# Block products in three feed-forward stages, and modulation sums on GpSimd

## The chip, the core and the metric

The kernel runs on one core of one Trainium2 chip. The metric is the device time of one execution, in microseconds. Below, PE is TensorE, PEld its weight loads, DVE is VectorE, ACT is ScalarE, POOL is GpSimd and SP is SyncE, which issues the loads of weights.

## The reference, cut to what matters

A sequence of 512 tokens of width 1024 passes through three transformer blocks in float32. Four of their stages are feed-forward ones; three matter here:

- `f1` and `f2`, at the start and at the end of the first block: `h = silu(x @ w_gate) * (x @ w_up)` with a hidden width of 2816, then `x = layernorm(alpha * x + 0.5 * (h @ w_down))`.
- `mlp`, at the end of the third block: `h = square(relu(x @ w1))` with a hidden width of 4096, then `x + gate * (h @ w2)` and a norm.

The modulation of the third block is a small product beside them: `mod = silu(c) @ ada_w + ada_b`, with `ada_w` of 1024 x 6144. It does not depend on x, so the kernel works it out long before the third block.

## The kernel before, in words

**Precision.** Every float32 matrix product is made of three products of a faster type. x and each weight are cut into a high and a low half: ACT copies to a rounded type (`w_high`, line 431), DVE subtracts (`w_low`, line 443), and PE sums low times high, high times low and high times high (lines 467 and 646). x is kept turned (`x_high`, `x_low`: 8 blocks of 128 rows by 512 tokens).

**A plain tile.** A unit of weights is 1024 rows by 128 columns (512 KB). It is loaded into one of the 4 slots of a ring (line 415); SP issues the loads in order, and load c waits until what slot c - 4 held is used up. ACT and DVE cut it, and PE runs 24 matmuls of 512 columns into one bank. In `f1` all 22 gate tiles and 22 up tiles are plain, in `mlp` all 32.

**A block pair (class `Seven`, lines 510 to 704).** The gate tile and the up tile of the same 128 hidden columns share x. As a two by two block problem (K in two halves, tokens in two halves of 256, the two tiles as the other side) they need eight block products, and a scheme of Strassen and Winograd needs seven: 1 and 2 with x as it is, 6, 5, 7 and 3 with sums of x blocks (`SH`, `SL`, made once for the stage), 4 with x as it is, in the order 1, 2, 6, 5, 7, 3, 4. Each is 12 matmuls of 256 columns. The weights need sums as well: DVE makes `t21` (lines 618 and 620) and `t43` (lines 627 and 628), which are then cut like any unit, so a pair has four units: w1, t21, t43, and the second half of w2. ACT copies four partial results out of the banks (line 683), DVE adds them up (c11, c22, c12: lines 690, 696, 703) and multiplies (line 1225). In the kernel before, only `f2` does this, for 16 of its 22 pairs (j = 6 to 21); the first 6 are plain.

DVE works through a pair in a written order (`vector_ffn_seven`): low of t43(p), t21(p+1), c11(p), low of w22(p), low of w1(p+1), low of t21(p+1), t43(p+1), c22(p), c12(p), the multiplication. A chunk w1 of the ring is free once t43 is made from it, w2 once the low half of w22 is made.

**Modulation (class `Ada`).** `ada_w` comes in 12 column groups of 512, each in four chunks of 512 KB through the same ring: (group i, quarter q). Per chunk DVE does two `scalar_tensor_tensor` of 128x512 into an accumulator (line 965; the first of a group is a `tensor_scalar`), and after the fourth PE sums over the partitions with four small matmuls (line 978, a "column set"), which DVE adds to the bias. Groups 0 to 10 lie in `f1`, one chunk behind each of its 44 tiles, group 11 in the first four tiles of `f2`.

**POOL** in `f1` and `f2` issues the loads of the norm's rows, scales x by alpha in four instructions (line 1245), and is then idle to the end of the stage. In `mlp` it squares each tile out of `f_relu` (line 4354).

**The end of each stage** is the down product: its units rotate through the 3 places of `w_high`/`w_low` and through extra places laid over memory that is free by then (`Down.place`).

Of the kernel before, what the change touches and what calls it, by code (L numbers as in the profile page):

```python
# [968 lines left out]
def tensor_ada_columns(b, a, i, accs):  # L969
    if not 0 <= i < 12:  # L970
        return
    pe, acc = b.nc.tensor, accs[i % 2]
# [3 lines left out]
    pe.wait_ge(*a.g.dve.at("acc", i, 3))  # L976
# [158 lines left out]
def scalar_ffn(b, s):  # L1135
    ac, g, last = b.nc.scalar, s.g, len(s.order) - 1
    tokens = scalar_seven_tokens(b, s.seven) if s.seven else None
    for m, (what, j) in enumerate(s.order):
        if m == last - 1 and not s.seven:
            scalar_down_begin(b, g, s.down, hid_ready(s))  # L1140
        scalar_ahead(b, (s.tag, m), min(AHEAD, last - m) if s.seven else AHEAD)
        if s.seven and m >= last - 1:
# [4131 lines left out]
```

## Time and profile before

| | us |
|---|---|
| median of 3 runs | 3454.5 (3451.12 to 3454.76) |
| the profiled execution | 3452.42 |
| its span | 3451.2 |

The span runs from the first to the last instruction; the execution's own time is 1.2 us longer. The profile lists busy time by engine and, for chosen stretches, by window. `f1` is from 9 to 263 us before its down product, `f2` from about 1128 to 1351 us, `mlp` from 3092 to 3275 us.

### The profile page before, as it was taken

How to read it: one execution, taken by the hardware profiler on the slowest of the kernel's cores; microseconds unless marked ns; L12 is line 12 of the kernel's file. 1: busy time of each engine (PE TensorE's matmuls, PEld its weight loads, DVE VectorE, ACT ScalarE, POOL GpSimd, SP SyncE). 2: the span in 40 equal slices, each digit the busy share in tenths (PEclk: the TensorE clock that was granted, in tenths of full speed). 3: DMA queues.
4: the chain of work that ended last, by engine and by line, in shares of the span. 5: the costliest groups of instructions: out<-in, count | busy, mean ns of one | idle time of the engine just before them, and what ended most of it. 6: DMA issues, size and time to landing. Idle time of an engine off the chain costs nothing. (4 is left out here: it accounts for less than half of the span.)

```text
span 3451.2 us, 45725 instructions
## 1 busy us (share of the span) xinstructions
PE 3381.5 (98%) x17532; PEld 2837.8 (82%) x17532; DVE 2106.2 (61%) x3344; ACT 1495.7 (43%) x2717; POOL 334.4 (10%) x374
## 2 busy tenths in 40 slices
PE   8999999999999999999999999999999999999999
PEld 7887888886777899887887788887787888888887
DVE  5456565678546787763344576667476577672266
ACT  3225344345443355546223363346255243452354
POOL 1000200003000100023010100000000104222100
PEclk9999999999999999999999999999999999999999
DMA  6556421220224334620322243245411320143365
GB/s 242 189 184 213 144 68 56 85 87 25 91 93 158 116 105 155 199 79 13 110 81 87 68 135 99 96 165 165 121 38 31 115 91 26 38 141 98 105 201 165
DMA packets 107974, 386.30 MB, mean 112 GB/s; under 512 B 12060, under 2 KB 14764, under 8 KB 107504
## 3 DMA queue, kind: packets, MB, share of 16 engines
q1 hardware_dynamic: 101088, 364.86, 32.2%
q0 software_dynamic: 4528, 16.43, 1.6%
q8 instruction: 142, 2.33, 0.3%
q10 hardware_dynamic: 2144, 2.10, 0.2%
q14 instruction: 72, 0.59, 0.1%
HBM read 379.13 MB, written 4.21 MB: 111 GB/s over the span
## 5 line engine op out<-in xcount | busy, mean ns | idle before, releaser
L443 DVE TENSOR_TENSOR w_low<-ring,w_high 128x1024 fp32r<-128x1024 f32 (+2 forms) x519 | 650.8, 1256 | 701.7 <-ACT w_high L431 693.9
L467 PE MATMUL bank<-x_low,w_high 128*128 128x512 f32 (+1 forms) x2144 | 828.8, 390 | 16.4 <-DVE w_low L443 10.1
L467 PE MATMUL bank<-x_high,w_low 128*128 128x512 f32 (+1 forms) x2144 | 814.9, 384 | 0.0
L431 ACT ACTIVATE w_high<-ring 128x1024 fp32r<-128x1024 f32 (+2 forms) x519 | 538.0, 1038 | 592.3 <-PE bank L467 243.1
L467 PE MATMUL bank<-x_high,w_high 128*128 128x512 f32 (+1 forms) x2144 | 528.4, 384 | 0.0
L467 PEld LDWEIGHTS bank<-x_low,w_high 128*128 128x128 f32 x2144 | 404.7, 189 | 96.0 <-issue 16.1
L467 PEld LDWEIGHTS bank<-x_high,w_low 128*128 128x128 f32 x2144 | 405.0, 189 | 74.9 <-issue 3.6
L467 PEld LDWEIGHTS bank<-x_high,w_high 128*128 128x128 f32 x2144 | 388.1, 189 | 77.2 <-issue 4.8
L737 PE MATMUL bank<-w_low,x_high 128*128 128x512 f32 (+1 forms) x384 | 145.5, 379 | 2.5 <-ACT z_z L2076 1.5
L739 PE MATMUL bank<-w_high,x_high 128*128 128x512 f32 (+1 forms) x384 | 143.5, 374 | 0.0
L738 PE MATMUL bank<-w_high,x_low 128*128 128x512 f32 (+1 forms) x384 | 143.5, 374 | 0.0
L737 PEld LDWEIGHTS bank<-w_low,x_high 128*128 128x128 f32 x384 | 72.1, 188 | 18.6 <-DVE w_low L443 2.7
L402 POOL DMA_DIRECT2D const<-in_consts x3 | 1.8, 589 | 834.0 <-DVE x_low L920 361.9
L739 PEld LDWEIGHTS bank<-w_high,x_high 128*128 128x128 f32 x384 | 72.1, 188 | 12.7
L738 PEld LDWEIGHTS bank<-w_high,x_low 128*128 128x128 f32 x384 | 72.1, 188 | 12.3 <-issue 0.2
L3061 ACT ACTIVATE c_in<-bank 128x512 f32<-128x512 f32 x44 | 26.4, 599 | 101.3 <-PE bank L467 101.2
L4335 ACT ACTIVATE f_relu<-bank 128x512 f32<-128x512 f32 x32 | 19.1, 598 | 116.6 <-PE bank L467 116.6
L3084 DVE SCALAR_TENSOR_TENSOR c_y<-c_in,cols,c_y 128x512 f32<-128x512 f32 x88 | 66.2, 752 | 3.1
L965 DVE SCALAR_TENSOR_TENSOR f_ada<-ring,cond,f_ada 128x512 f32<-128x512 f32 x84 | 65.4, 778 | 2.8
L851 PE MATMUL bank<-w_low,c2d_in 128*128 128x512 f32 x168 | 65.7, 391 | 0.0
L853 PE MATMUL bank<-w_high,c2d_in 128*128 128x512 f32 x168 | 65.4, 389 | 0.0
L852 PE MATMUL bank<-w_high,c2d_in 128*128 128x512 f32 x168 | 65.3, 389 | 0.0
(746 smaller groups left out, 6917.8 us busy)
## 6 DMA issues: line engine op xcount, KB each, us to landing
ring<-in_W SPq DMA_DIRECT2D x686, 512.0 KB, 3.5
X<-in_x POOLq DMA_DIRECT2D x1, 2048.0 KB, 10.9
x_spill<-X POOLq DMA_DIRECT2D x1, 2048.0 KB, 8.3
X<-x_spill POOLq DMA_DIRECT2D x4, 512.0 KB, 3.6
ring<-in_W SPq DMA_DIRECT2D x4, 432.0 KB, 3.2
out<-X SPq DMA_DIRECT2D x3, 512.0 KB, 5.0
const<-in_consts POOLq DMA_DIRECT2D x1, 1133.0 KB, 10.6
f_hid<-in_xT ACTq DMA_DIRECT2D x4, 256.0 KB, 8.1
```

Of the source, the lines that this page charges most:

```text
L431: ac.activation(b.UH[u.place][:, 0:u.K * u.n], u.src(), ACT.Copy).then_inc(*b.split.act.up("high", i))
L443: dv.tensor_tensor(b.UL[u.place][:, 0:n], u.src(), b.UH[u.place][:, 0:n].bitcast(F32), SUB).then_inc(*b.split.dve.up("low", i))
L467: i = pe.matmul(out, w[:, k, c], v, start=n == 0 and q == 0, stop=last and q == 3 * K - 1)
L737: pe.matmul(out, xh, wl[:, q, :], start=k + q == 0, stop=False)
L738: pe.matmul(out, xl, wh[:, q, :], start=False, stop=False)
L739: i = pe.matmul(out, xh, wh[:, q, :], start=False, stop=k + q == 7)
L851: pe.matmul(out, u[:, 0, s], wl[:, 0, c], start=k == 0, stop=False)
L852: pe.matmul(out, u[:, 1, s], wh[:, 0, c], start=False, stop=False)
L853: x = pe.matmul(out, u[:, 0, s], wh[:, 0, c], start=False, stop=k == d.nk - 1)
L965: x = dv.scalar_tensor_tensor(acc, w[:, k, :], b.cond[:, 2 * q + k:2 * q + k + 1], acc, MUL, ADD)
L3061: ac.activation(s.cb[m % 3][:, 2:514], b.bk["c2u", m], ACT.Copy).then_inc(*g.act.up("copied", m))
L3084: dv.scalar_tensor_tensor(y, x[:, q:q + 512], b.col("ffn_conv_w_2", 44 * q + c), y, MUL, ADD).then_inc(*(g.dve.up("conv", m) if q == 2 els ...
```

## The change

- `f1` and `mlp` use block pairs too: `f1` has 6 plain pairs and 16 block pairs as `f2` has, `mlp` has 6 plain tiles and then 13 pairs of neighbouring tiles (j and j + 1).
- In `mlp` POOL makes the four whole blocks of x that the sums need, DVE the sums; the relu of a pair is done in place in `hid` by three ACT instructions, and POOL squares the pair's two tiles in place behind the last of them. The operands of the last product (`Down.H`), the norm's row and the places of `mlp` lie over the memory of the sums, and wait for the last pair's products. The norm's row is loaded behind the last pair.
- Modulation: `f1` has groups 0 to 5, `f2` groups 6 to 11. The first two groups of each stage ("early") are summed on DVE beside the first 8 plain tiles as before. The other four ("late") are summed on POOL, one chunk per block pair: per quarter chunk row block a `tensor_scalar` into `product` and a `tensor_tensor` that adds it to the accumulator, both of 128x512. Their column sets stand behind pairs 5, 9 and 13, the last one in the down product. Accumulator and product lie in the memory of the norm's rows, so these are loaded when the last column set is done.
- The ring's order in the block pairs of `f1` and `f2` is now w1, w2, modulation chunk, so w2(p+1) needs the slot of w1(p), and w1(p+1) needs the slot of modulation chunk p - 1.

```diff
+def gpsimd_ada_step(b, a, i, q, acc, tmp, over):
+
+    gp, w = b.nc.gpsimd, b.w(("ada", i, q))
+    gp.wait_ge(*b.loaded(("ada", i, q)))
+    if q == 0:
+        gp.wait_ge(*a.g.act.at("cond"))
+        if over is not None:
+            gp.wait_ge(*a.g.pe.at("columns", over))
+        gp.tensor_scalar(acc, w[:, 0, :], b.cond[:, 0:1], None, MUL).then_inc(*a.pool.up())
+    for k in range(0 if q else 1, 2):
+        gp.tensor_scalar(tmp, w[:, k, :], b.cond[:, 2 * q + k:2 * q + k + 1], None, MUL).then_inc(*a.pool.up())
+        gp.wait_ge(*a.pool.now())
+        x = gp.tensor_tensor(acc, acc, tmp, ADD)
+        x.then_inc(*(a.pool.up("acc", i, q) if k else a.pool.up()))
+        gp.wait_ge(*a.pool.now())
+
...
+PLAIN = 3
...
+        self.acc = {i: copies[:, 512 * (n % 2):512 * (n % 2) + 512] for n, i in enumerate(early)}
+        self.acc.update({i: self.G[:, 0, 512 * (n % 2):512 * (n % 2) + 512] for n, i in enumerate(late)})
+        self.over = {i: x[n - 2] if n > 1 else None for x in (early, late) for n, i in enumerate(x)}
+        self.product = self.G[:, 1, 0:512]
...
+        self.seven = Seven(b, Area(b, self.end), self.g, f"{tag}s", copies)
...
+    def early_steps(self, m):
+
+        return [(self.early[m // 4], m % 4)] if 0 <= m < 4 * len(self.early) else []
+
+    def early_columns(self, m):
+
+        return {7: self.early[:1], 11: self.early[1:]}.get(m, [])
+
+    def late_columns(self, p):
+
+        return self.late[(p - 5) // 4] if p in (5, 9, 13) else None
...
 def ffn_units(b, s, before=None):
     s.first = FIRST if before else NU
+    last = len(s.order) - 1
     for m, (what, j) in enumerate(s.order):
         b.unit((s.tag, m), (s.pre + "_w_gate", s.pre + "_w_up"), down_rows(8), [(j * 128 + what * 2816, 128)],
                lambda m=m: s.g.pe.at(s.tag, m))
-        for q in (m - 1,) if 0 < m < 43 else (42, 43) if m == 43 else ():
-            ada_chunk(b, s.ada, s.ada_from + q // 4, q % 4)
+        for q in (m - 1, m) if m == last else (m - 1,):
+            for step in s.early_steps(q):
+                ada_chunk(b, s.ada, *step)
         if before and m == FIRST - 1:
             leave_places(b, before)
     for j in range(s.plain, 22):
         seven_units(b, s.seven, (s.pre + "_w_gate", s.pre + "_w_up"), j * 128, 2816 + j * 128)
+        p = j - s.plain
+        if p < 4 * len(s.late):
+            ada_chunk(b, s.ada, s.late[p // 4], p % 4)
     down_units(b, s.g, s.down, s.pre + "_w_down")
-    if s.seven:
-        s.down.added.append(s.seven.added)
+    s.down.added.append(s.seven.added)
...
-        if m % 4 == 3 and m > 3:
-            tensor_ada_columns(b, s.ada, s.ada_from + m // 4 - 1, s.acc)
+        for i in s.early_columns(m):
+            tensor_ada_columns(b, s.ada, i, s.acc[i])
     for p in range(22 - s.plain):
         tag = s.seven.tag
         tensor_seven(b, s.seven, p, {"p": g.act.at("silu", s.plain + p), "q": g.dve.at(tag, "c11", p),
                                      "r": g.dve.at(tag, "c12", p)})
+        i = s.late_columns(p)
+        if i is not None:
+            tensor_ada_columns(b, s.ada, i, s.acc[i])
...
 def gpsimd_ffn(b, s, ready):
     gp, g = b.nc.gpsimd, s.g
-    for i, what in enumerate("gb"):
-        gp.dma_start(s.G[:, i, :], b.io[f"{s.norm}_{what}"].partition_broadcast(128)).then_inc(
-            b.load_sem(f"{s.norm}{what}"), 16)
     for t in range(4):
         for r in ready(t):
             gp.wait_ge(*r)
         gp.tensor_scalar(b.X[:, t, :], b.X[:, t, :], ALPHA, None, MUL).then_inc(*g.pool.up("alpha", t))
+    for i in s.late:
+        for q in range(4):
+            gpsimd_ada_step(b, s.ada, i, q, s.acc[i], s.product, s.over[i])
+    gp.wait_ge(*s.ada.g.pe.at("columns", s.late[-1]))
+    for i, what in enumerate("gb"):
+        gp.dma_start(s.G[:, i, :], b.io[f"{s.norm}_{what}"].partition_broadcast(128)).then_inc(
+            b.load_sem(f"{s.norm}{what}"), 16)
...
-    for m in range(32):
+    for m in range(SINGLE):
...
+    for m in range(SINGLE, 32, 2):
+        seven_units(b, s.seven, "mlp_w1_3", 128 * m, 128 * m + 128)
...
+SINGLE = 6
+LAST_PAIR = (32 - SINGLE) // 2 - 1
...
+def gpsimd_mlp_whole(b, s, n):
+
+    i, j = ((0, 0), (1, 0), (1, 1), (0, 1))[n]
+    b.nc.gpsimd.tensor_tensor(s.seven.work[n], block(b.XH, i, j).bitcast(F32), block(b.XL, i, j).bitcast(F32),
+                              ADD).then_inc(*s.gm.pool.up("whole", n))
...
+def scalar_mlp_pair(b, s, p):
+    ac, g, v, j = b.nc.scalar, s.gm, s.seven, SINGLE + 2 * p
+    scalar_ahead(b, (v.tag, "t43", p), 0)
+    if p == 0:
+        ac.wait_ge(*g.pool.at("hid", SINGLE - 1))
+    scalar_seven_copy(b, v, p, "a", 1, "p", "c11")
+    scalar_ahead(b, (v.tag, "w22", p), 0)
+    scalar_ahead(b, mlp_behind(s, p, 0), 0)
+    scalar_seven_copy(b, v, p, "b", 6, "p", "c12")
+    scalar_seven_copy(b, v, p, "d", 5, "r", "c22")
+    if p == LAST_PAIR:
+        scalar_down_begin(b, s.gf, s.downf, mlp_ready(s))
+    scalar_ahead(b, mlp_behind(s, p, 1), 0)
+    scalar_seven_copy(b, v, p, "c", 7, "p", "c22")
+    x = s.hid[:, j, 0:256]
+    ac.wait_ge(*g.dve.at(v.tag, "c11", p))
+    ac.activation(x, x, ACT.Relu).then_inc(*g.act.up())
+    ac.wait_ge(*g.pe.at(v.tag, 4, p))
+    ac.activation(s.hid[:, j, 256:512], b.bk[v.tag, "p", p][:, 0:256], ACT.Relu).then_inc(*g.act.up(v.tag, "c21", p))
+    x = s.hid[:, j + 1, :]
+    ac.wait_ge(*g.dve.at(v.tag, "c12", p))
+    ac.activation(x, x, ACT.Relu).then_inc(*g.act.up("pair", p))
...
+def vector_mlp_pair(b, s, p):
+    v, j = s.seven, SINGLE + 2 * p
+    vector_ahead(b, (v.tag, "t43", p), 0)
+    if p < LAST_PAIR:
+        vector_seven_t21(b, v, p + 1)
+    if p == LAST_PAIR:
+        b.nc.vector.wait_ge(*b.split.dve.at("low", b.unit_of[v.tag, "t43", p]))
+    vector_seven_c11(b, v, p, s.hid[:, j, 0:256])
+    vector_ahead(b, (v.tag, "w22", p), 0)
+    vector_ahead(b, mlp_behind(s, p, 1), 0)
+    if p < LAST_PAIR:
+        vector_seven_t43(b, v, p + 1)
+    vector_seven_c22(b, v, p, s.hid[:, j + 1, 256:512])
+    vector_seven_c12(b, v, p, s.hid[:, j + 1, 0:256])
+    if p == LAST_PAIR:
+        vector_down_begin(b, s.gf, s.downf)
...
+    for p in range(LAST_PAIR + 1):
+        gp.wait_ge(*g.act.at("pair", p))
+        for j in (SINGLE + 2 * p, SINGLE + 2 * p + 1):
+            x = s.hid[:, j, :]
+            gp.tensor_tensor(x, x, x, MUL).then_inc(*g.pool.up("hid", j))
+    gp.wait_ge(*g.pe.at(s.seven.tag, 4, LAST_PAIR))
+    gp.dma_start(s.GF, b.io["final_g_3"].partition_broadcast(128)).then_inc(b.load_sem("final_g_3"), 16)
...
-        self.f1 = Ffn(b, self.ada, "f1", "ffn1", "ln1", 0)
+        self.f1 = Ffn(b, self.ada, "f1", "ffn1", "ln1", [0, 1], [2, 3, 4, 5])
+        self.ada.pool = self.f1.g.pool
         self.staged = self.f1.hid[:, 14:22, :]
         self.m1 = Mix1(b)
-        self.f2 = Ffn(b, self.ada, "f2", "ffn2", "ln3", 11, 3)
+        self.f2 = Ffn(b, self.ada, "f2", "ffn2", "ln3", [6, 7], [8, 9, 10, 11])
...
```

## Rows read from the trace of the kernel before

**Rows 1.** Part 1 of the page: busy time of each engine.
```profile
PE 3381.5 (98%) x17532; PEld 2837.8 (82%) x17532; DVE 2106.2 (61%) x3344; ACT 1495.7 (43%) x2717; POOL 334.4 (10%) x374
```

**Rows 2.** Windows: us, busy us (count) of PE, PEld, DVE, ACT, POOL, clock, DMA.
```profile
59.22:240.92 181.70, 181.70 (x834) 151.30 (x834) 94.17 (x121) 42.63 (x48) 0.00 (x0) 1.00 0.51 185
1204.90:1341.60 136.70, 136.70 (x1179) 136.70 (x1178) 119.91 (x169) 80.02 (x140) 0.00 (x0) 1.00 0.34 109
```

**Rows 3.** Chain that ended last, in order of time: start us, us, what.
```profile
3017.40 27.22 PE bank L467 x120
```

**Rows 4.** Timeline of DVE in one block pair: start us, us, what, idle before.
```profile
1202.33 1.23 DVE L443 TENSOR_TENSOR w_low<-f2s_t,w_high 128x1024 fp32r<-128x1024 f32 x1 [1.53 <-ACT w_high L431]
1203.59 0.69 DVE L627 TENSOR_TENSOR f2s_t<-ring,f2s_t 128x512 f32<-128x512 f32 x1
1204.20 0.68 DVE L628 TENSOR_TENSOR f2s_t<-ring 128x512 f32<-128x512 f32 x1
1204.80 0.42 DVE L696 TENSOR_TENSOR f_hid<-f_ada 128x256 f32<-128x256 f32 x1
1205.13 0.42 DVE L703 TENSOR_TENSOR f_hid<-bank,f_ada 128x256 f32<-128x256 f32 x1
1205.59 0.69 DVE L1225 TENSOR_TENSOR f_hid<-f_hid,f_gate 128x512 f32<-128x512 f32 x1
1206.47 1.23 DVE L443 TENSOR_TENSOR w_low<-f2s_t,w_high 128x1024 fp32r<-128x1024 f32 x1 [0.18 <-ACT w_high L431]
1207.83 0.69 DVE L618 TENSOR_TENSOR f2s_t<-ring,ring 128x512 f32<-128x512 f32 x1
1208.56 0.69 DVE L620 TENSOR_TENSOR f2s_t<-ring,f2s_t 128x512 f32<-128x512 f32 x1
1209.16 0.42 DVE L690 TENSOR_TENSOR f_gate<-bank,f_ada 128x256 f32<-128x256 f32 x1
1209.50 0.68 DVE L443 TENSOR_TENSOR w_low<-ring,w_high 128x512 fp32r<-128x512 f32 x1
1210.10 1.22 DVE L443 TENSOR_TENSOR f2s_unit<-ring,f2s_unit 128x1024 fp32r<-128x1024 f32 x1
1212.15 1.23 DVE L443 TENSOR_TENSOR w_low<-f2s_t,w_high 128x1024 fp32r<-128x1024 f32 x1 [0.83 <-ACT w_high L431]
```

**Rows 5.** Timeline of PE in the next block pair (product 3, next product 1).
```profile
1211.88 0.28 PE L646 MATMUL bank<-f2s_sl,w_high 128*128 128x256 f32 x1
...
1214.66 0.28 PE L646 MATMUL bank<-x_low,f2s_unit 128*128 128x256 f32 x1
```

**Rows 6.** Page, part 6: one load of the ring, KB, us to landing.
```profile
ring<-in_W SPq DMA_DIRECT2D x686, 512.0 KB, 3.5
```

**Rows 7.** Timelines at 1020 us: an adding instruction of POOL beside DVE.
```profile
1020.24 1.29 POOL L1422 TENSOR_TENSOR m_merged<-m_merged,bs_part 128x512 f32<-128x512 f32 x1 [8.76 <-DVE bs_part L1409]
...
1020.62 1.99 DVE L443 TENSOR_TENSOR w_low<-ring,w_high 128x1024 fp32r<-128x1024 f32 x1 [0.46 <-ACT w_high L431]
```

**Rows 8.** Timelines of the first stage, POOL beside DVE at 28 and 32 us.
```profile
28.34 2.80 POOL L1245 TENSOR_SCALAR X<-X 128x1024 f32<-128x1024 f32 x1 [8.95 <-DMA X<-in_x]
...
28.34 1.59 DVE L965 SCALAR_TENSOR_TENSOR f_ada<-ring,cond,f_ada 128x512 f32<-128x512 f32 x1
...
31.12 2.76 POOL L1245 TENSOR_SCALAR X<-X 128x1024 f32<-128x1024 f32 x1
...
32.23 1.23 DVE L443 TENSOR_TENSOR w_low<-ring,w_high 128x1024 fp32r<-128x1024 f32 x1 [1.51 <-ACT w_high L431]
```

**Rows 9.** Source line 965: duration ns min/median/max, first and last start, forms.
```profile
L965 DVE SCALAR_TENSOR_TENSOR f_ada<-ring,cond,f_ada x84: 741/752/1592, 20.0 to 1154.9; 128x512 f32<-128x512 f32 x84
```

**Rows 10.** Source line 4354: the squares on POOL in the third stage.
```profile
L4354 POOL TENSOR_TENSOR f_hid<-f_relu x32: 1031/1042/1042, 3110.0 to 3270.9; 128x512 f32<-128x512 f32 x32
```

**Rows 11.** Timeline of ACT behind product 4 of a block pair.
```profile
1205.11 0.38 ACT L1178 ACTIVATE f_gate<-bank 128x256 f32<-128x256 f32 x1 [2.09 <-PE bank L646]
1205.39 1.05 ACT L431 ACTIVATE w_high<-f2s_t 128x1024 fp32r<-128x1024 f32 x1
```

More of the change, by code:

```diff
@@ L515, in __init__ @@
         self.SL = area.take(f"{tag}_sl", 4, 4, 256, dtype=F32R, past=3 * LINE)
-        self.T = area.take(f"{tag}_t", 1024)
-        area = place_area or area
+        self.T = area.take(f"{tag}_t", 1024) if T is None else T
         over = Area(b, area.at)
-        self.place = [area.take(f"{tag}_unit", SLOT, dtype=F32R) for _ in range(2)]
-        self.work = [self.T.rearrange("p (k c) -> p k c", k=4)] + [over.take(f"{tag}_x", 4, 256) for _ in range(2)]
+        self.place = [area.take(f"{tag}_unit", SLOT, dtype=F32R, past=LINE) for _ in range(2)]
+        self.work = list(work) or [four(self.T)] + [over.take(f"{tag}_x", 4, 256) for _ in range(2)]
         self.copy = {x: copies[:, 256 * i:256 * i + 256] for i, x in enumerate("abcd")}
@@ L975, in tensor_ada_columns @@
         pe.wait_ge(*e)
[L976 removed]
+    pe.wait_ge(*a.acc(i, 3))
     for j in range(4):
@@ L1136, in scalar_ffn @@
     ac, g, last = b.nc.scalar, s.g, len(s.order) - 1
-    tokens = scalar_seven_tokens(b, s.seven) if s.seven else None
+    tokens = scalar_seven_tokens(b, s.seven)
     for m, (what, j) in enumerate(s.order):
[L1139 to L1142, printed above, removed]
+        scalar_ahead(b, (s.tag, m), min(AHEAD, last - m))
+        if m >= last - 1:
             scalar_seven_start(b, s.seven, m == last)
@@ L1220, in vector_ffn_seven @@
             vector_seven_t43(b, v, p + 1)
+        for i in s.early_columns(len(s.order) - 1) if p == 0 else ():
+            vector_ada_columns(b, s.ada, i)
+        i = s.late_columns(p - 1)
+        if i is not None:
+            vector_ada_columns(b, s.ada, i)
         vector_seven_c22(b, v, p, s.hid[:, j, 256:512])
@@ L4323, in tensor_mlp, with vector_mlp_sum, summed, scalar_mlp_high @@
         tensor_tile(b, g, ("f3u", m), [("f3u", m)], 0, b.x, bank.ap)
-def scalar_mlp(b, s):
-    ac, g = b.nc.scalar, s.gm
-    for m in range(32):
-        if m == 30:
-            scalar_down_begin(b, s.gf, s.downf, mlp_ready(s))
-        scalar_ahead(b, ("f3u", m))
+    for p in range(LAST_PAIR + 1):
+        tensor_seven(b, s.seven, p, {"p": g.act.at(tag, "c21", p), "q": g.dve.at(tag, "c11", p),
+                                     "r": g.dve.at(tag, "c12", p)})
+def gpsimd_mlp_whole(b, s, n):
+    i, j = ((0, 0), (1, 0), (1, 1), (0, 1))[n]
+    b.nc.gpsimd.tensor_tensor(s.seven.work[n], block(b.XH, i, j).bitcast(F32), block(b.XL, i, j).bitcast(F32),
+                              ADD).then_inc(*s.gm.pool.up("whole", n))
+def vector_mlp_sum(b, s, i):
+    dv, g, f, tag, (w0, w1, w2, w3, w4) = b.nc.vector, s.gm, s.gm.dve, s.seven.tag, s.seven.work
+    out, one, two, op, n = {2: (w4, w0, w1, SUB, 1), 0: (w1, w1, w2, ADD, 2), 1: (w0, w1, w0, SUB, 2),
+                            3: (w3, w3, w0, SUB, 3)}[i]
+    dv.wait_ge(*g.pool.at("whole", n))
+    if i != 2:
+        dv.wait_ge(*f.now())
+    dv.tensor_tensor(out, one, two, op).then_inc(*f.up(tag, "sum", i))
+def summed(s, i):
+    w0, w1, w2, w3, w4 = s.seven.work
+    return {2: w4, 0: w1, 1: w0, 3: w3}[i]
+def scalar_mlp_high(b, s, i):
+    ac, g, v = b.nc.scalar, s.gm, s.seven
+    ac.wait_ge(*g.dve.at(v.tag, "sum", i))
+    ac.activation(v.SH[:, i, :, :], summed(s, i), ACT.Copy).then_inc(*g.act.up(v.tag, "high", i))
+def vector_mlp_low(b, s, i):
+    dv, g, v = b.nc.vector, s.gm, s.seven
+    dv.wait_ge(*g.act.at(v.tag, "high", i))
+    dv.tensor_tensor(v.SL[:, i, :, :], summed(s, i), v.SH[:, i, :, :].bitcast(F32),
+                     SUB).then_inc(*g.dve.up(v.tag, "low", i))
+def scalar_mlp(b, s):
+    ac, g, v, last = b.nc.scalar, s.gm, s.seven, SINGLE - 1
+    for m in range(SINGLE):
+        scalar_ahead(b, ("f3u", m), min(AHEAD, last - m))
+        if m >= last - 1:
+            scalar_ahead(b, (v.tag, "t21" if m == last else "w1", 0), 0)
         ac.wait_ge(*g.pe.at("f3u", m))
@@ L4338, in mlp_ready @@
 def mlp_ready(s):
-    return lambda k: [s.gm.pool.at("hid", k)]
+    g, tag = s.gm, s.seven.tag
+    return lambda k: [g.pool.at("hid", k)] + ([g.pe.at(tag, 5 if k < 3 else 4, LAST_PAIR)] if k < 4 else [])
 def vector_mlp(b, s):
-    for m in range(32):
-        vector_ahead(b, ("f3u", m))
-        if m == 30:
-            vector_down_begin(b, s.gf, s.downf)
+    dv, g, v, last = b.nc.vector, s.gm, s.seven, SINGLE - 1
+    sums, lows = {1: (2,), 2: (0, 1), 3: (3,)}, {4: (2, 0), 5: (1, 3)}
+    for m in range(SINGLE):
+        vector_ahead(b, ("f3u", m), min(AHEAD, last - m))
+        for i in sums.get(m, ()):
+            vector_mlp_sum(b, s, i)
+        if m == last - 2:
+            dv.wait_ge(*g.pe.at("f3u", FIRST - 1))
+            vector_seven_t21(b, v, 0)
+        for i in lows.get(m, ()):
+            vector_mlp_low(b, s, i)
+        if m >= last - 1:
+            vector_ahead(b, (v.tag, "t21" if m == last else "w1", 0), 0)
```

129 lines of the change are left out of this document (70 added, 59 removed).

## The prediction

> **What bounds the kernel now.** I read part 1 of the page first: PE is busy for 98% of the span [rows 1]. So only what takes work off PE, or makes PE wait, moves the time. Then I compared two stretches by window: in the plain tiles of `f1` and in the block pairs of `f2` PE is busy without a gap, at the full clock (1.00, the 2.4 GHz level), while POOL does nothing at all [rows 2]. What differs is DVE: 94.17 of 181.70 us in the plain tiles, although modulation runs on it, but 119.91 of 136.70 us, 88%, in the block pairs. So the block pair is cheaper on PE and is close to being bound by DVE. The reader is to see in the timeline of one pair how little is left: two idle pieces, 0.83 and 0.18 us [rows 4].
>
> **What a pair costs.** Plain: five tiles (120 matmuls) take 27.22 us in the chain [rows 3], so 5.44 a tile, 10.89 a pair. Block pair: 14 of them in 136.70 us [rows 2] are 9.76 each. The change turns 16 pairs of `f1` and 13 pairs of `mlp` into block pairs: if nothing else moved, that would be 29 x 1.13 = 32.7 us off PE. The column sets of modulation: the first stretch of rows 2 is 8 times four tiles with one set, 22.71 us each, less 4 x 5.444 = 21.78 leaves 0.93 us a set. There are 12 before and after.
>
> **What is added, and where.** In 16 pairs of `f1` and in 16 of `f2`, POOL sums a modulation chunk: two `tensor_scalar` and two adding `tensor_tensor` of 128x512 (a first quarter has one of the latter, so 1.75 on average). Alone they would be nothing to PE. The question is what they do to DVE, whose 88% I have just named. The rows on this:
> - An adding instruction of POOL of this size and form takes 1.29 us. DVE's low half begins 0.38 us after it and takes 1.99 instead of 1.23 [rows 7, 4]: it is held up for 0.76, until 1.14 us after POOL's start. So an add holds DVE off for 1.14 us.
> - A `tensor_scalar` of 128x1024 takes 2.80 us. DVE's `f_ada` instruction that starts with it takes 1.59 instead of 0.75 [rows 8, 9], so it is held off for 0.84 us, but a low half that starts 1.1 us after the next one takes 1.23 as if alone [rows 8]. Half the size: an estimate of 0.42 us.
> - The instructions that suffer read two operands from SBUF. In a block pair that is all of DVE's work but c11 and c12, which read a bank [rows 4].
>
> The Trainium skill ("SBUF — State Buffer", section "Who interferes with whom") says that DVE with two SBUF inputs and a GpSimd instruction that reads SBUF contend for one shared pair of ports, and that the one which comes second fully blocks. It speaks of a lock for the whole instruction; the low half at 32.23 us, 1.23 long inside a 2.76 us instruction of POOL, disagrees with "whole" [rows 8], the add agrees nearly. It is a rule against this change, and its full form is rival D.
>
> So per chunk POOL holds DVE off for up to 2 x 0.42 + 1.75 x 1.14 = 2.84 us. DVE's own work in a pair, from start to start with the two idle pieces taken out, is 9.76 - 1.01 = 8.75 [rows 2, 4]. Were all of the hold-off paid: 11.6 us. Part of it falls beside c11, c12 (0.34 each from start to start) and the short waits between dependent instructions, and part of an instruction's hold is hidden when DVE's next start would come later anyway. Walking POOL's four instructions through rows 4 from the landing of a chunk, I get 2.3 for a chunk with four and 1.6 for a first quarter: 2.15 on average. **Period P in `f1` and `f2`: 8.75 + 2.15 = 10.9 us**, taken as 10.95 with small change; bounds 9.76 (all hidden) and 11.6 (none). DVE is then what ends last: PE waits for the low half of w22, product 3's weights. Today that half ends at 1210.18 (1209.50 + 0.68) and product 3 begins at 1211.88 [rows 4, 5], so DVE can fall behind by 1.7 us once before PE waits.
>
> Nothing else is late in this loop: ACT has the room, and a load takes 3.5 us [rows 6]. w2 of the pair after next is issued when t43 is made (1204.20 + 0.68) and would land at 1208.4, 0.6 us after t21 starts today (1207.83) [rows 4]; the 0.83 of idle covers it, and in a DVE-bound pair the hold-off between the two does. POOL needs some 2 x (1.4 + 1.3) = 5.4 us for a chunk and with its own blocking some 7.5, less than a period, so its slot of the ring comes back in time.
>
> **The sum.** The first chunk of a stage is summed before pair 0, so 15 periods are stretched: 15 x (10.95 - 9.76) - 1.7 = 16.1 us per stage.
> - `f1`: 16 x 9.76 + 16.1 - 16 x 10.89 = -1.9 us.
> - `f2`: already block pairs, so the loss alone: +16.1 us.
> - Column sets: the three late ones of each stage stand where PE waits for DVE, so 6 x 0.93 = 5.6 us are hidden: -5.6 us.
> - `mlp`: no modulation, but two squares a pair. One takes 1.04 us [rows 10] and holds DVE off by an estimated 0.9. DVE has no multiplication here, so its work is 8.75 - 0.8 = 7.95. The longest loop: behind product 4 (0.0) relu of the bank to 0.6, of the second tile 0.6 to 1.2 (one of 128x512, an estimate from 0.38 for half of it), high of t43 to 2.3 [rows 11], the second square in the way until 3.2, low 4.4, t21 5.8, c11 6.1, w22 low 6.8, and product 3 wants it at 1211.88 - 1204.90 = 6.98. It just fits; I take 9.80 a pair: 13 x (10.89 - 9.80) = -14.2 us. At worst the loop overruns: 10.5 a pair, -5.1.
> - Start and end of `mlp`: eight splits of sums on ACT and DVE have 13.8 us of PE work (two tiles, two products) in front of product 6 and need some 11; at the end ACT cuts three operands before the last copy c, about 0.5 us late. +1.5 in all, bounds 0 and 6. In `f1` and `f2` the start is that of `f2` today, where PE goes from plain tiles into pairs without a gap; four more modulation steps on DVE (1.5 us each) lie in plain tiles with DVE half free. 0.
> - Loads of the norm's rows later, extra places that wait for the last products, POOL's four whole blocks: 0, each with tens of us of down product or tiles over it; bound 1.
>
> -1.9 + 16.1 - 5.6 - 14.2 + 1.5 = **-4.1 us**. The terms are differences inside the span (3451.2), to which the execution adds 1.2: 3452.4 - 4.1 = 3448.3. The median of the runs is 2.1 above that execution (0.06%): **3450.4 us**. This is a draw: 0.2%, 6.9 us, is about the least that a measurement of this kernel can tell from no change. By P the total goes as 30 us per us of period (15 x 2), and it crosses zero at P = 11.1.
>
> **The rivals.**
> - **A. POOL mostly hides (faster).** If POOL's instructions come to run where DVE is waiting anyway, or find gaps between its instructions without holding it, P falls to 9.76 to 10.5. For it: 1.01 idle per pair, and both engines are regular. Against: one add alone is longer than both idle pieces. At 10.3: 15 x 0.54 - 1.7 = 6.4 a stage: -11.6 + 6.4 - 5.6 - 12.7 = -23.5, 3431 us. With no contention at all the sets are not hidden: -18.1 + 0 - 14.7 + 1.5 = -31, 3423 us.
> - **B. The hold-offs are paid in full (slower).** The mechanism is that DVE's instructions stand one behind the other, so that each hold shifts all that follow; P = 8.75 + 2.84 = 11.6, and `mlp` overruns too (10.5). 15 x 1.84 - 1.7 = 25.9: +7.9 + 25.9 - 5.6 - 5.1 + 1.5 = +24.6, 3479 us; with `mlp` at 9.80, 3470. It decides from P = 11.1. For it: the rows show DVE instructions delayed by the full remainder of POOL's hold. Against: c11, c12 and the waits must hide something.
> - **C. The change hardly does what it says on DVE:** if the chunk's slot came back late, w1 and w2 would land late and the ring would set the period. Its price is the excess over 3 us of margin; the trace of before can't show POOL's duration under load. It adds to B; 12 us a period would be +27 us, 3481.
> - **D. The other's whole instruction.** 2 x 1.4 + 1.75 x 1.29 = 5.1 a chunk, less 0.5: P = 13.3, 51 us a stage: +34 + 51 - 5.6 - 12.7 = +67, 3521 us. The rule of the skill's page named above, taken literally, gives it; rows 8 speak against it.
>
> **How the numbers follow.** The forecast (P between 10.7 and 11.3, 3443 to 3461) 0.35; A 0.34; B 0.24; C 0.04; D 0.03. The range leaves out no contention at all (3423), C's tail and D: 3427 to 3477. Faster by over 0.2% (under 3447.6): all of A and a small part of the forecast, 0.37; slower (over 3461.4): B, C, D, 0.32; within, 0.31.
>
> **What would show it.** In the profile after: windows over the block pairs of `f1` and `f2` should give some 10.95 us a pair with DVE at 95% or more and PE at about 89%; PE idle before products of line 646 should be put down to DVE line 443 (`w_low<-ring`, w22). The mean of DVE's `tensor_tensor` with two SBUF operands there should be up by about a quarter, c11 and c12 unchanged. `mlp` should be at 9.8 a pair without gaps. I would be wrong in the mechanism if PE had no idle in these pairs, if its waits were for ACT or the ring, or if `mlp`'s block pairs were the slow ones.

## The result and the profile after

The changed kernel takes **3474.7 us** (median of 6 runs, 3471.3 to 3477.7) against 3454.2 for the kernel before (6 runs beside it). The ratio is 1.0059, with a 95% interval of 1.0048 to 1.0070: slower by 20.5 us. The forecast was 3450, a draw.

Part 1 of the page, to be read beside [rows 1]: PE is busy for 9.4 us less, yet the span is 21.6 us longer (3472.8). So PE has 31 us more without work. POOL has 246 us more work.
```profile
PE 3372.1 (97%) x18576; PEld 2871.4 (83%) x18576; DVE 2305.8 (66%) x3561; ACT 1590.8 (46%) x2928; POOL 580.0 (17%) x498
```
Windows over 14 block pairs of `f1`, 14 of `f2` and 11 of `mlp` (columns as in [rows 2]):
```profile
93.35:248.09 154.74, 145.06 (x1202) 143.19 (x1201) 140.24 (x172) 80.29 (x140) 94.97 (x53) 0.98 0.42 144
1204.71:1358.85 154.14, 142.83 (x1202) 140.15 (x1201) 141.74 (x172) 80.44 (x140) 98.01 (x53) 1.00 0.44 145
3166.53:3278.49 111.96, 110.85 (x926) 108.88 (x925) 91.46 (x120) 67.26 (x121) 33.33 (x22) 1.00 0.33 104
```
A pair of `f2` took 9.76 in the kernel before. It now takes 154.14 / 14 = 11.01, one of `f1` 11.05 and one of `mlp` 10.18 (111.96 / 11). These are means: by the starts of product 1, single pairs of `f1` take 9.8 to 13.6 and of `f2` 9.8 to 12.0. DVE is busy 140.24 / 14 = 10.02 us per pair instead of 119.91 / 14 = 8.57 [rows 2], for the same instructions. But it isn't busy all the time: 14.5 us of the first window are idle. What ended the idle time over much the same stretch of `f1` (engine, what waited, for what; us in total, times, longest):
```profile
POOL f_norm L977 <- DMA ring<-in_W: 62.3, 12, 17.2
...
DVE f1s_t L617 <- DMA ring<-in_W: 11.0, 10, 2.4
PE bank L645 <- DVE w_low L443: 9.5, 8, 1.9
```
PE waits for the low half of w22, as forecast. DVE itself waits for t21, which needs w2 from the ring. That wait was not in the forecast. A stretch of DVE in `f1` shows both (start us, us, what, idle before), to be read beside [rows 4]:
```profile
159.54 0.69 DVE L627 TENSOR_TENSOR f1s_t<-ring 128x512 f32<-128x512 f32 x1
...
161.65 1.21 DVE L443 TENSOR_TENSOR w_low<-f1s_t,w_high 128x1024 fp32r<-128x1024 f32 x1
164.51 0.84 DVE L617 TENSOR_TENSOR f1s_t<-ring,ring 128x512 f32<-128x512 f32 x1 [1.65 <-DMA ring<-in_W]
...
166.33 1.44 DVE L443 TENSOR_TENSOR w_low<-ring,w_high 128x512 fp32r<-128x512 f32 x1
167.69 1.21 DVE L443 TENSOR_TENSOR f1s_unit<-ring,f1s_unit 128x1024 fp32r<-128x1024 f32 x1
...
188.76 2.31 DVE L443 TENSOR_TENSOR f1s_unit<-ring,f1s_unit 128x1024 fp32r<-128x1024 f32 x1
```
and POOL beside it:
```profile
162.15 1.87 POOL L979 TENSOR_TENSOR f_norm<-f_norm 128x512 f32<-128x512 f32 x1
164.12 1.57 POOL L977 TENSOR_SCALAR f_norm<-ring,cond 128x512 f32<-128x512 f32 x1
165.77 1.45 POOL L979 TENSOR_TENSOR f_norm<-f_norm 128x512 f32<-128x512 f32 x1
...
188.33 1.66 POOL L979 TENSOR_TENSOR f_norm<-f_norm 128x512 f32<-128x512 f32 x1
```
The load of w2 goes out when t43 is made (159.54 + 0.69 = 160.23, SP's issue is at 160.25) and lands at 164.43, so it takes 4.2 us. DVE is ready 1.65 us earlier, at 162.86, since little held it off between t43 and t21: POOL is at work there too, but t43's low half takes 1.21, what it takes alone. The next three loads of w2 took 4.9, 3.4 and 3.6 us, and even behind the one of 3.4 DVE waited 0.95. Then the low half at 166.33 takes 1.44 instead of 0.68, beside an add of POOL, and the one at 188.76 takes 2.31 instead of 1.22.

The longest pair of `f1`, 13.6 us, has a wait of PE of 1.90 us that ends at 123.70. PE's matmuls then start 0.12 us apart to 124.7, 0.21 apart to 127.9 and 0.12 apart again, and the granted clock shows it (columns as above):
```profile
124.00:128.00 4.00, 4.00 (x25) 4.00 (x24) 3.79 (x6) 0.00 (x0) 0.92 (x1) 0.62 0.69 262
```

**Ledger** of the two profiled executions, by first matmuls (us; difference after minus before):

| stretch | before | after | difference | forecast |
|---|---|---|---|---|
| start to first product of `f1`'s down | 254.5 | 248.8 | -5.7 | } |
| `f1`'s down product | 125.4 | 128.0 | +2.6 | } |
| to the first block pair of `f2` | 806.1 | 807.6 | +1.5 | } +8.6 |
| 16 block pairs of `f2` | 156.1 | 175.1 | +19.0 | } |
| `f2`'s down product | 122.5 | 124.3 | +1.8 | } |
| from there to `mlp` | | | -0.1 | 0 |
| `mlp`'s tiles and pairs | 178.6 | 179.2 | +0.6 | -12.7 |
| `mlp`'s down product | 173.9 | 176.2 | +2.3 | 0 |

Five column sets (0.93 each) that stood in the first row's stretch before stand in `f2` now: one right ahead of its first block pair (at 1192.67, so in the third row), three in its pairs and one in its down product. The rows sum to +22.0, with marks slightly inside the span's ends.

### The profile page after: what moved, and what is told of

It is laid out like the page before. It is cut to its first block and busy times, and to the rows that moved or that the text cites. A ratio compares the mean times of both kernels' runs of the same rounds, so it can differ in the third digit from the quotient of the medians.

```text
span 3472.8 us, 48745 instructions
## 1 busy us (share of the span) xinstructions
PE 3372.1 (97%) x18576; PEld 2871.4 (83%) x18576; DVE 2305.8 (66%) x3561; ACT 1590.8 (46%) x2928; POOL 580.0 (17%) x498
## 5 line engine op out<-in xcount | busy, mean ns | idle before, releaser
L443 DVE TENSOR_TENSOR w_low<-ring,w_high 128x1024 fp32r<-128x1024 f32 (+1 forms) x481 | 602.0, 1253 | 525.3 <-ACT w_high L431 517.5
L431 ACT ACTIVATE w_high<-ring 128x1024 fp32r<-128x1024 f32 (+1 forms) x481 | 485.1, 1010 | 496.2 <-PE bank L467 209.3
L467 PE MATMUL bank<-x_low,w_high 128*128 128x512 f32 (+1 forms) x1712 | 656.3, 389 | 17.9 <-DVE w_low L443 11.2
L467 PE MATMUL bank<-x_high,w_low 128*128 128x512 f32 (+1 forms) x1712 | 642.9, 381 | 0.0
L467 PE MATMUL bank<-x_high,w_high 128*128 128x512 f32 (+1 forms) x1712 | 418.2, 381 | 0.0
L467 PEld LDWEIGHTS bank<-x_low,w_high 128*128 128x128 f32 x1712 | 324.3, 189 | 80.1 <-issue 16.0
L467 PEld LDWEIGHTS bank<-x_high,w_low 128*128 128x128 f32 x1712 | 324.7, 190 | 57.0 <-issue 3.6
L467 PEld LDWEIGHTS bank<-x_high,w_high 128*128 128x128 f32 x1712 | 305.1, 189 | 59.1 <-issue 4.8
L977 POOL TENSOR_SCALAR f_norm<-ring,cond 128x512 f32<-128x512 f32 x56 | 111.8, 1997 | 126.6 <-DMA ring<-in_W 124.3
L979 POOL TENSOR_TENSOR f_norm<-f_norm 128x512 f32<-128x512 f32 x56 | 90.6, 1619 | 4.7
L738 PEld LDWEIGHTS bank<-w_high,x_high 128*128 128x128 f32 x384 | 72.1, 188 | 12.7
```

What stands on the lines that cost most here:

```text
L431: ac.activation(b.UH[u.place][:, 0:u.K * u.n], u.src(), ACT.Copy).then_inc(*b.split.act.up("high", i))
L443: dv.tensor_tensor(b.UL[u.place][:, 0:n], u.src(), b.UH[u.place][:, 0:n].bitcast(F32), SUB).then_inc(*b.split.dve.up("low", i))
L467: i = pe.matmul(out, w[:, k, c], v, start=n == 0 and q == 0, stop=last and q == 3 * K - 1)
L738: i = pe.matmul(out, xh, wh[:, q, :], start=False, stop=k + q == 7)
L977: gp.tensor_scalar(tmp, w[:, k, :], b.cond[:, 2 * q + k:2 * q + k + 1], None, MUL).then_inc(*a.pool.up())
L979: x = gp.tensor_tensor(acc, acc, tmp, ADD)
```

## The experiments

Each ratio is to the kernel before, timed beside it.

**tiny_sums.** The changed kernel with POOL's late sums cut to one column; loads, waits and order of the instructions stay, and POOL clears the accumulators' row once at the start of each stage. Left out: the other 511 columns of these sums.
```
-        gp.tensor_scalar(acc, w[:, 0, :], b.cond[:, 0:1], None, MUL).then_inc(*a.pool.up())
+        gp.tensor_scalar(acc[:, 0:1], w[:, 0, 0:1], b.cond[:, 0:1], None, MUL).then_inc(*a.pool.up())
...
-        x = gp.tensor_tensor(acc, acc, tmp, ADD)
+        x = gp.tensor_tensor(acc[:, 0:1], acc[:, 0:1], tmp[:, 0:1], ADD)
```


> The changed kernel with POOL's modulation instructions in the block pairs cut to one column (128x1 in place of 128x512): loads, ring and waits stay, the modulation that it computes for groups 2 to 5 and 8 to 11 is not the reference's. Theory PORT (POOL's instructions hold DVE off): the period of a block pair in f1 and f2 falls from 11.0 to 9.8 to 10.1 us, the time from 3474.7 to about 3442 (30 periods x 1.05, less some column sets that are no longer hidden). Rival RING (w2 of the next pair waits for the slot of w1, so the load sets the period): the period stays above 10.7, the time above 3465.

Measured: 3440.9 us, ratio 0.9964 (0.9951 to 0.9977). A window over `f1`'s pairs, and what DVE waited for in it:
```profile
93.00:240.00 147.00, 146.99 (x1273) 146.82 (x1272) 126.52 (x184) 86.08 (x152) 31.94 (x57) 1.00 0.47 161
...
DVE f1s_t L617 <- DMA ring<-in_W: 12.7, 14, 1.4
```
The pair is back at 9.7 to 9.8 (10.5 where a column set stands in it), and PE has no gap. DVE waits for the ring as long as in the changed kernel, 12.7 us, and it costs nothing. So it is POOL's work on full tiles, 33.8 us in all (3474.7 - 3440.9), that makes the change slow; the ring's lateness by itself does not.

**sums_no_loads.** The same sums at full size, but on constants and started when t43 of the pair is made; the 32 late chunks are not loaded. Left out: the late chunks as data.
```
-    gp, w = b.nc.gpsimd, b.w(("ada", i, q))
-    gp.wait_ge(*b.loaded(("ada", i, q)))
+    gp, w = b.nc.gpsimd, bc(b.cx[0][:, 0:512], 1, 2)
+    gp.wait_ge(*pace)
...
-        if p < 4 * len(s.late):
-            ada_chunk(b, s.ada, s.late[p // 4], p % 4)
```


> The counterpart: POOL runs the same 128x512 instructions at the same places, but on the constants; the 32 late chunks are not loaded (that part of the modulation is not the reference's), so the ring has two loads a pair as f2 had before. PORT alone: the period stays at 10.9 to 11.0, the time about 3473. RING: the period falls to 9.8 to 10.1, about 3442. If both act, one behind the other in the loop of DVE: about 10.6, 3463.

Measured: 3463.8 us, ratio 1.0032 (1.0019 to 1.0044); the profiled execution was at 3458.3. DVE waits for nothing that the waits' view lists, and is full:
```profile
93.00:240.00 147.00, 141.94 (x1185) 138.54 (x1185) 143.72 (x169) 79.41 (x140) 93.02 (x53) 1.00 0.29 97
...
L617 DVE TENSOR_TENSOR f1s_t<-ring,ring x16: 686/1568/1579, 75.9 to 235.5; 128x512 f32<-128x512 f32 x16
```
The second line is the duration of t21's first instruction (ns, min/median/max): 1568 in the median, where the kernel before has 693. A pair takes some 10.65 (10.7 to 11.1, a first quarter 10.2). The hold-off alone is thus worth about 0.9 us a pair over 9.76, and the loads add 0.35 on top of it. The split holds only roughly, since POOL's instructions stand at a fixed place of the pair here and not in the changed kernel.

**dve_sums.** The late sums on DVE, behind the last multiplication of the pair: no hold-off, but 1.45 us of DVE's own.
```
         dv.tensor_tensor(s.hid[:, j, :], s.hid[:, j, :], s.gate[j % 3], MUL).then_inc(*g.dve.up("hid", j))
+        i = s.late[p // 4]
+        vector_ada_step(b, s.ada, i, p % 4, s.acc[i], s.over[i])
```


> The late modulation sums on DVE (two scalar_tensor_tensor a pair, 1.5 us) behind the pair's multiplication, nothing on POOL. PORT: DVE's work is 8.75 + 1.45 = 10.2 us and nothing holds it off, so 10.3 to 10.5 a pair, 3474.7 - 30 x 0.6 = about 3457. RING: DVE is as late with t43 and the load as before, 10.9 to 11.2, about 3475 or more.

Measured: 3564.2 us, ratio 1.0322 (1.0307 to 1.0338). That is 107 us over the 3457 of the first theory, and the pairs of `f1` behind the first took 12.6 to 17.9. DVE is less busy than before, and SP, which issues the loads, waits for the sums (L963):
```profile
93.00:240.00 147.00, 112.19 (x901) 108.30 (x900) 101.39 (x148) 58.56 (x106) 0.00 (x0) 0.98 0.34 115
...
DVE f1s_t L617 <- DMA ring<-in_W: 42.3, 11, 5.0
...
SPq L415 <- DVE f_norm L963: 74.5, 12, 7.9
```
and in its timeline:
```profile
178.59 1.53 DVE L963 SCALAR_TENSOR_TENSOR f_norm<-ring,cond,f_norm 128x512 f32<-128x512 f32 x2
180.04 1.22 DVE L443 TENSOR_TENSOR w_low<-f1s_t,w_high 128x1024 fp32r<-128x1024 f32 x1
184.64 0.69 DVE L617 TENSOR_TENSOR f1s_t<-ring,ring 128x512 f32<-128x512 f32 x1 [3.38 <-DMA ring<-in_W]
```
The chunk is used up at 180.1 only. w1 of the pair whose t21 comes next needs its slot, and w2 stands behind that w1 in SP's order: SP issues the two at 180.16 and 180.5, the second lands 4.0 us later, and t21 starts at 184.64. That delays the next chunk's use in turn. This is rival C, made by hand: its mechanism exists and is the most expensive of all that were run.

**mlp_plain.** The changed kernel with the stage `mlp` of the kernel before, single tiles and squares as they were.
```
-    for m in range(SINGLE, 32, 2):
-        seven_units(b, s.seven, "mlp_w1_3", 128 * m, 128 * m + 128)
...
-    for m in range(SINGLE):
+    for m in range(32):
```


> The changed kernel with mlp as before (32 plain tiles). By the trace mlp up to its down product takes 179.2 us in place of 178.6, and its down product 176.2 in place of 173.9, so block pairs there now cost 3 us in all: 3472. Had mlp gained what was forecast (12.7 us), this kernel would be at 3487.

Measured: 3471.7 us, ratio 1.0055 (1.0040 to 1.0070). `mlp`'s block pairs gain nothing; they cost 3.0 us (3474.7 - 3471.7; the ranges of the two kernels' runs overlap).

**mlp_pairs_alone.** The other way round: the kernel before with only `mlp`'s part of the change.
```
-    for m in range(32):
+    for m in range(SINGLE):
...
+    for m in range(SINGLE, 32, 2):
+        seven_units(b, s.seven, "mlp_w1_3", 128 * m, 128 * m + 128)
```


> The kernel before with the change's block pairs in mlp alone (f1, f2 and modulation as before). By the ledger of the two traces mlp is then 0.6 us slower up to its down product and 2.3 in it: 3456 us against 3453.4 of the kernel before. By the forecast's term (-12.7) it would be 3441.

Measured: 3455.7 us, ratio 1.0004 (0.9995 to 1.0014). That is 1.4 us for `mlp`'s part alone, and 3.0 for it in the changed kernel; the two are the same within the noise. My sum had -12.7 for this kernel.

**mlp_wholes_dve.** As the last, with the four whole blocks of x added by DVE instead of POOL.
```
-def gpsimd_mlp_whole(b, s, n):
+def vector_mlp_whole(b, s, n):
...
-    dv.wait_ge(*g.pool.at("whole", n))
-    if i != 2:
-        dv.wait_ge(*f.now())
+    dv.wait_ge(*f.now())
```


> As mlp_pairs_alone, with the four whole blocks of x made by DVE at the stage's start in place of POOL. Theory START (POOL's 2.4 us instructions and DVE's sums hold each other off, and PE waits 6.5 us before tile 4, product 1 and product 6): about 6 us less, 3450. Rival: DVE has 4.9 us more to do before the same deadline, and PE waits as long: 3456.

Measured: 3449.9 us, ratio 0.9989 (0.9980 to 0.9999), 5.8 us less; two of its ten runs took 3455.1 and 3457.5, the others 3447.7 to 3450.8. How POOL's wholes stood in the way is in the changed kernel's timelines, POOL first:
```profile
3125.89 7.12 POOL L4381 TENSOR_TENSOR f_hid<-x_high,x_low 128x1024 f32<-128x1024 f32 x3 [11.73 <-DVE x_low L2277]
3132.97 2.03 POOL L4508 TENSOR_TENSOR f_hid<-f_relu 128x512 f32<-128x512 f32 x1
3134.96 3.38 POOL L4381 TENSOR_TENSOR f_hid<-x_high,x_low 128x1024 f32<-128x1024 f32 x1
```
```profile
3130.78 3.32 DVE L4393 TENSOR_TENSOR f_hid<-f_hid 128x1024 f32<-128x1024 f32 x1 [5.12 <-POOL f_hid L4381]
3134.02 2.06 DVE L443 TENSOR_TENSOR w_low<-ring,w_high 128x1024 fp32r<-128x1024 f32 x1
```
DVE first waits 5.12 us for two blocks, 2.4 each, and then its sums of 1.2 take up to 3.3 beside POOL. PE pays three times, at tile 5's low half, at product 1's weights and at copy a (start us, us, what, idle before):
```profile
3143.53 0.47 PE L467 MATMUL bank<-x_low,w_high 128*128 128x512 f32 x1 [1.47 <-DVE w_low L443]
...
3151.09 0.36 PE L645 MATMUL bank<-x_low,f3s_unit 128*128 128x256 f32 x1 [1.84 <-DVE f3s_unit L443]
...
3157.94 0.39 PE L645 MATMUL bank<-f3s_sl,w_high 128*128 128x256 f32 x1 [2.69 <-ACT f_relu L682]
```
With DVE's wholes the first two are gone and the third is 3.2. From the last `o_in` product to `mlp`'s down product it takes 174.9 instead of 179.4, so 4.5 less for 2.5 less of waiting. What the stalls cost beyond themselves is the clock. Windows of mlp_squares_act before, in and behind its one stall of 3.2 us:
```profile
3129.30:3132.20 2.90, 2.90 (x25) 2.76 (x23) 2.90 (x3) 0.60 (x1) 1.47 (x1) 1.00 0.02 6
3132.20:3135.40 3.20, 0.06 (x1) 0.00 (x0) 2.04 (x4) 1.34 (x3) 0.00 (x0) 1.00 0.03 10
3135.44:3138.10 2.66, 2.66 (x16) 2.66 (x17) 2.49 (x4) 1.81 (x3) 0.00 (x0) 0.69 0.48 185
3138.10:3140.10 2.00, 2.00 (x12) 2.00 (x12) 1.90 (x3) 0.00 (x0) 0.00 (x0) 0.56 0.16 31
3140.10:3144.20 4.10, 4.10 (x37) 4.10 (x37) 2.69 (x4) 2.02 (x4) 0.00 (x0) 1.00 0.32 113
```
Once the work is back the granted clock is 0.69 and then 0.56 in the mean. In the rows of PE, matmuls start 0.12 us apart to 3136.5, 0.21 apart to 3139.9 (the level of 1.2 GHz) and 0.12 apart again (2.4 GHz). PE has 28 records in 4.66 us where the next window has 37 in 4.10. At that rate the 28 are worth 3.1 us, so about 1.6 us is lost behind a stall of 3.2. In the changed kernel the clock is 0.70 in the 3.7 us behind 3151.09.

**mlp_squares_act.** As the last, with the squares of a pair's tiles on ACT, one pair later.
```
+        ac.activation(x, x, ACT.Square).then_inc(*g.act.up("hid", j))
...
-            gp.tensor_tensor(x, x, x, MUL).then_inc(*g.pool.up("hid", j))
```


> As mlp_wholes_dve, with the squares of a pair done by ACT one pair later, where it waits for product 4. Theory SQUARES (the second square holds DVE's t21 off for 0.6 us, and the loop relu, relu, high of t43, low, t21, w22 overruns): the period of mlp falls from 10.24 to 9.76, 12 x 0.48 = 5.8 us, to about 3444. Rival: the loop through ACT alone (relu of 512 columns behind c12) is too long, the period stays above 10.1: 3450.

Measured: 3444.9 us, ratio 0.9972 (0.9961 to 0.9983), another 5.0 us less. The loop that the pair period hung on, in the changed kernel, ACT, then DVE, then POOL:
```profile
3207.03 0.39 ACT L4453 ACTIVATE f_hid<-bank 128x256 f32<-128x256 f32 x1 [2.09 <-PE bank L645]
3207.99 0.63 ACT L4456 ACTIVATE f_hid<-f_hid 128x512 f32<-128x512 f32 x1 [0.57 <-DVE f_hid L702]
3208.53 1.04 ACT L431 ACTIVATE w_high<-f_hid 128x1024 fp32r<-128x1024 f32 x1
```
```profile
3209.60 1.23 DVE L443 TENSOR_TENSOR w_low<-f_hid,w_high 128x1024 fp32r<-128x1024 f32 x1 [1.65 <-ACT w_high L431]
3210.96 1.31 DVE L617 TENSOR_TENSOR f_hid<-ring,ring 128x512 f32<-128x512 f32 x1
3212.31 0.69 DVE L619 TENSOR_TENSOR f_hid<-ring,f_hid 128x512 f32<-128x512 f32 x1
```
```profile
3208.70 3.03 POOL L4515 TENSOR_TENSOR f_hid<-f_hid 128x512 f32<-128x512 f32 x2 [7.21 <-ACT f_hid L4456]
```
The relu of the second tile waits for c12 and starts 0.96 us behind the first relu, where I had 0.6. POOL's second square ends at 3211.73 and stretches t21 from 0.69 to 1.31. That shifts all of DVE's work behind it, c12 too, so the loop runs: c12, relu, high of t43, low of t43, t21, and through DVE's rest of the pair to c12. What PE waits for in it is not a low half but copy a, which ACT has behind the high of t43: PEld's waits over `mlp`'s pairs, then copy a and the first matmul of product 6.
```profile
PEld bank L645 <- ACT f_relu L682: 2.9, 9, 0.4
...
3209.47 0.37 ACT L682 ACTIVATE f_relu<-bank 128x256 f32<-128x256 f32 x1
...
3209.89 0.39 PE L645 MATMUL bank<-f3s_sl,w_high 128*128 128x256 f32 x1
```
Copy a ends at 3209.84, and product 6 starts 3.06 us behind product 1 (3206.83) where it takes 2.83 in mlp_squares_act. There the relus stand as they did, but c12 ends 0.72 us behind the start of product 1 and not 1.12. So taking the squares off POOL is enough to shorten the loop, with the relus left in their order. With the squares on ACT a pair takes 9.71, and PE is busy for all of 100 us:
```profile
3150.00:3250.00 100.00, 100.00 (x868) 100.00 (x867) 81.31 (x114) 75.31 (x136) 0.00 (x0) 1.00 0.36 111
```

**dve_early.** The changed kernel with both edits of `mlp`, and with the late sums on DVE as in dve_sums, but ahead of t21 and not at the pair's end.
```
         vector_ahead(b, (v.tag, "t43", p), 0)
+        i = s.late[p // 4]
+        vector_ada_step(b, s.ada, i, p % 4, s.acc[i], s.over[i])
         if p + 1 < 22 - s.plain:
             vector_seven_t21(b, v, p + 1)
```


> The changed kernel with both mlp edits, and with the late modulation sums on DVE, this time ahead of t21 in the pair (dve_sums had them last). Theory SLOT: in dve_sums w1 of the pair after next waited for the slot of this pair's chunk until the pair's end, and w2 behind it in SP's order, so t21 waited for a load in each pair (13.8 us a pair). Early, the slot is back before w2 is due, and the period is DVE's work, 10.2 to 10.4 us: about 3442 to 3446. Rival: DVE's instructions themselves are the price (two more of them with semaphore waits each), and the period stays over 11: 3465 or more.

Measured: **3431.1 us**, ratio 0.9931 (0.9916 to 0.9945): 23 us faster than the kernel before and 44 faster than the changed one. The expectation was 3442 to 3446. Windows over the pairs of `f1` and `f2`, and a piece of one pair on DVE:
```profile
93.00:240.00 147.00, 146.68 (x1265) 146.46 (x1264) 143.83 (x212) 86.05 (x152) 0.00 (x0) 1.00 0.45 158
1184.00:1333.00 149.00, 148.06 (x1275) 147.55 (x1274) 145.00 (x215) 86.97 (x153) 0.00 (x0) 1.00 0.47 159
```
```profile
1206.93 1.22 DVE L443 TENSOR_TENSOR w_low<-f2s_t,w_high 128x1024 fp32r<-128x1024 f32 x1
1208.07 1.53 DVE L963 SCALAR_TENSOR_TENSOR f_norm<-ring,cond,f_norm 128x512 f32<-128x512 f32 x2
1209.51 0.69 DVE L617 TENSOR_TENSOR f2s_t<-ring,ring 128x512 f32<-128x512 f32 x1
```
The sums fill the time in which DVE would wait for the ring: of the 11.0 us of such waits in the changed kernel, one of 0.3 is left. From the fifth pair of a stage on, most pairs take 9.70 to 9.79, or 10.5 to 10.9 with a column set; the first four take 9.8 to 10.5. In the windows DVE is busy for 98 and 97%, PE for 99.8 and 99.4%. It is the same work as in dve_sums, at another place of the pair: the two kernels are 133 us apart, 11 of them from `mlp` (3455.7 - 3444.9), so 122 from the place.

## Why the prediction was wrong

- **What bounds the pair: right.** In `f1` and `f2` DVE becomes the bound, PE waits for the low half of w22 (9.5 us over 8 waits in `f1`), and the cause is POOL's work. tiny_sums shows that with POOL's instructions cut to one column the change is at 3440.9.
- **The period: right in size, composed differently.** Forecast 10.95, measured 11.0. The hold-offs were put at 2.15 us a pair; DVE's busy time rose by 10.02 - 8.57 = 1.45, and 1.55 in `f2`. The rest of the period is DVE waiting for w2, 11.0 / 14 = 0.8 us a pair. "Nothing else is late in this loop" failed here. The walk saw that w2 would land 0.6 us after t21's start, and left it to the hold-off between t43 and t21 to cover that; in the timeline of DVE above, no hold-off falls there, and w2's load takes 3.4 to 4.9 us against 3.5 in [rows 6]. This is not rival C: SP waits for POOL's last add only 5 times in `f1`'s pairs, 4.0 us in all, and w2's issue follows t43. Two errors cancelled, so that the period came out right is in part luck.
- **The lag of 1.7 us: not seen.** I took it off once a stage as what DVE can fall behind for free. 16 pairs of `f1` took 174.8 where the forecast's terms give 172.3: 0.8 from the period, 1.7 this. `f2` took 175.1.
- **The column sets: as forecast in sum,** as far as the ledger closes. With the pairs 5.4 us over, the stretch from the start to the end of `f2`'s down product is 10.6 over its forecast. The rest: 1.2 in `f1`'s plain tiles (74.0 against 72.8), 2.6 in its down product, 0.6 of the +1.5 (the other 0.9 is the column set that now stands there) and 0.9 of the +1.8. The first two belong to the one execution: dve_early has 72.9 in the plain tiles, and mlp_plain, with the same `f1`, has 125.3 in the down product, where PE waits 0.5 us for `f1d_in` and not 1.9.
- **`f2`'s down product** has a term that I had at 0. In stretches without a wait, 60 of its matmuls take 13.60 us in the kernel before and 13.69 in every kernel with a part of the change, 0.8 us over 528 matmuls. mlp_pairs_alone has it too, where `f2` has its old instructions and only places in memory differ; its pairs in turn take 9.71 instead of 9.76. Why the place matters is open.
- **`mlp`: the step that failed.** Its term was -12.7 (13 x (10.89 - 9.80), less 1.5 for start and end), and it measured +0.6. These 13.3 us are over half of the 25.7 by which the executions missed the sum; 10.6 are the stages above, 2.3 the down product behind. The runs show two causes and a rest.
  First, "+1.5 in all, bounds 0 and 6": PE stood still for 6.0 us at the start, and the clock fell behind it. The tiles ahead took 3.8 us more than without POOL's blocks, and the first pair took 15.4. The cause of the waits in the tiles and ahead of product 1 is that DVE waited for POOL's whole blocks of 2.4 and was then held off by the last of them and by the squares (mlp_wholes_dve: -5.8, of which 4.5 in `mlp` up to its down product). I counted PE's 13.8 us of work against 11 of splits, without POOL's blocks in front and without a hold-off, although [rows 7, 8] give it.
  Second, "it just fits": the loop overran, with 10.24 a pair instead of 9.80. The walk had the second square in the way of the low half of t43 only, and that half was not held (1.23 us); the second square lay over t21, and c12 and the relu behind it came late (mlp_squares_act: -5.0, of which 5.7 in `mlp` up to its down product). The forecast's own worst case, 10.5 a pair, was the nearer one.
  Put on top of mlp_pairs_alone, the two edits give back 10.2 of the 13.3 us: `mlp` up to its down product goes from 179.4 to 169.2. The rest is mainly the first pair, which still takes 14.9: PE waits 3.2 us for copy a and runs slower behind it.
- **`mlp`'s down product** is 1.3 to 2.6 us longer in every kernel with block pairs there. I had a bound of 1 for its places over the sums' memory. The traces give most of the 2.3: in the changed kernel PE waits 1.1 us in it for `f3d_in`, the operand that lies over the sums (0.3 in mlp_squares_act), and 60 matmuls take 13.68 us where they take 13.60 with plain tiles ahead, 1.0 us over its 768 matmuls.
- **With its -12.7 from `mlp`** the kernel would be at 3474.7 - 13.3 = 3461.4, still 11 us above the forecast and just on the line that I had drawn to slower. The other stages have the rest of the miss.
- **The rivals.** A was refuted by the changed kernel itself (the periods), B came nearest in its total (3470 to 3479) but not in its mechanism: the hold-offs were paid to 1.5 of 2.84 a pair. D is out: it needs 13.3 a pair. The rule of the Trainium skill ("SBUF — State Buffer", section "Who interferes with whom") that one of the two engines waits out the other's instruction is borne out in its kind. Its size is mixed: the low half of 128x1024 at 188.76 takes 1.09 us more where POOL's add had 1.23 left to run, nearly all of it, but over a pair DVE pays 1.5 us for 6.8 us of POOL's work (94.97 / 14).

Open: in mlp_squares_act PE still waits 3.2 us once, at pair 0, for copy a. ACT has it behind the high half of t43, which waits 3.99 us for DVE. Putting copy a first was not tried. Its gain is not shown; the product behind the next needs t43's low half, which ends at 3136.4 there, only 1.0 us after PE goes on. dve_early, at 3431.1, has that wait too.

## What to carry to other kernels

Before GpSimd gets work beside a VectorE that is near its limit, look at what it does to VectorE: here 6.8 us of POOL's work cost DVE 1.5 us a pair, as much as doing the sums on DVE itself (1.45), and DVE could do these where it waited anyway. In a ring whose loads are issued in order, the place at which a chunk is used up counts more than the engine that uses it up: the same two instructions at the end of the pair cost 122 us more than ahead of t21. And the start of a stage is to be walked instruction by instruction as the steady loop is, with each instruction's own last input, not the one before it in the queue.
